# Five Strassen groups behind the keys and nine filler chunks in a written-out second attention

## The reference

```python
h = rms_norm(x, norm1_g)
q, k, v, bg, cg, xc = split(h @ w_in)            # 6 x 1024 columns
y_attn = chunked_relpos_attention(q, k, v, ...)  # 16 heads of 64, chunks of 64,
                                                 # each sees itself and 8 earlier ones
y_conv = bg * (conv_b + causal width-3 conv of cg * xc)
gates  = sigmoid(h @ w_gate + b_gate)            # 2 x 1024 columns
x = x + (g_attn * (y_attn @ w_attn_proj) + g_conv * (y_conv @ w_conv_proj)) @ w_out
```

## Time and profile before

| | before |
|---|---|
| runs | 2168.96, 2170.98, 2181.47 us, median 2170.98 |
| the profiled execution | 2173.93 us, span 2172.1 us |
| PE busy | 2145.6 us, 99% |
| DVE, ACT, POOL busy | 1472.0, 949.6, 998.3 us |
| instructions | 29103 |

### The profile page before, as it was taken

One profiled execution on the slowest core, in us unless ns is written; L12 is line 12 of the kernel. 1 busy time (PEld: TensorE's weight loads), 2 busy tenths in 40 slices (PEclk: granted clock), 3 DMA queues, 4 the chain that ended last, 5 costly groups with the idle time before them and its releaser, 6 DMA issues.

```text
span 2172.1 us, 29103 instructions
## 1 busy us (share of the span) xinstructions
PE 2145.6 (99%) x10450; PEld 1788.2 (82%) x10450; DVE 1472.0 (68%) x2585; ACT 949.6 (44%) x1696; POOL 998.3 (46%) x701
## 2 busy tenths in 40 slices
PE   8999999999998999999999999999999999999999
PEld 8888888888887888888888888788878887888887
DVE  7776775265874666666666658543776777898886
ACT  5555425343342555555555531212555454433332
POOL 3232465454644131322223147457466565556564
PEclk9999999999999999999999999999999999999999
DMA  7320124332226332323333256315143545826433
GB/s 231 105 76 21 45 91 152 126 117 97 87 88 176 89 108 69 112 72 104 88 93 88 69 195 241 107 49 194 49 154 140 171 146 185 319 93 228 150 122 115
DMA packets 198606, 269.34 MB, mean 124 GB/s; under 512 B 58136, under 2 KB 116280, under 8 KB 198368
## 3 DMA queue, kind: packets, MB, share of 16 engines
q1 hardware_dynamic: 124880, 201.38, 27.5%
q10 hardware_dynamic: 73616, 66.49, 10.0%
HBM read 191.23 MB, written 85.00 MB: 127 GB/s over the span
## 4 chain that ended last, share of the span: by engine, by line
PE 76%; DVE 9%; ACT 5%; DMA 4%; issue 4%; POOL 1%; ACTq 1%; DVEq 0%; SPq 0%; POOLq 0%
PE ps L204 64%; PE ps L2379 3%; DMA w_raw<-in_w_up_dram 2%; PE ps L2354 2%; PE ps L2366 2%; DVE res L3476 1%; DVE mlp_acc L3476 1%; PE ps L776 1%; DMA u_parts<-res 1%; PE ps L751 1%; PE ps L762 1%; DVE k_lo L2599 1%; ACT w_hi L3323 1%; DVE a_lo L446 1%; DVE mlp_acc L3464 1%
## 5 line engine op out<-in xcount | busy, mean ns | idle before, releaser
L204 PE MATMUL ps<-a_hi,w_hi 128*128 128x512 f32 x1376 | 536.9, 407 | 7.4 <-DVE res L2149 5.1
L159 POOL TENSOR_TENSOR w_hi<-w_raw,zero 128x512 fp32r<-128x512 f32 x172 | 203.5, 1214 | 735.6 <-PE ps L204 604.9
L204 PE MATMUL ps<-a_hi,w_lo 128*128 128x512 f32 x1376 | 516.6, 392 | 0.0
L204 PE MATMUL ps<-a_lo,w_hi 128*128 128x512 f32 x1376 | 514.0, 390 | 0.0
L204 PE MATMUL ps<-w_hi,a_hi 128*128 128x512 f32 (+1 forms) x960 | 368.5, 384 | 4.1 <-POOL w_lo L672 2.2
L204 PE MATMUL ps<-w_hi,a_lo 128*128 128x512 f32 (+1 forms) x960 | 367.1, 382 | 0.0
L204 PE MATMUL ps<-w_lo,a_hi 128*128 128x512 f32 (+1 forms) x960 | 366.8, 382 | 0.0
L204 PEld LDWEIGHTS ps<-a_hi,w_lo 128*128 128x128 f32 x1376 | 258.4, 188 | 57.7
L204 PEld LDWEIGHTS ps<-a_hi,w_hi 128*128 128x128 f32 x1376 | 258.8, 188 | 50.8 <-POOL w_lo L1923 5.5
L204 PEld LDWEIGHTS ps<-a_lo,w_hi 128*128 128x128 f32 x1376 | 259.8, 189 | 40.8
L164 POOL TENSOR_TENSOR w_lo<-w_raw,w_hi 128x512 fp32r<-128x512 f32 x172 | 243.4, 1446 | 3.4
(11 more groups left out here) (307 smaller groups left out, 3929.9 us busy)
## 6 DMA issues: line engine op xcount, KB each, us to landing
mlp_part<-u_parts SPq DMA_DIRECT2D x26, 1024.0 KB, 7.9
w_raw<-in_w_in_dram SPq DMA_DIRECT2D x24, 1024.0 KB, 5.3
feat_fm<-stage ACTq DMA_DIRECT2D x68, 256.0 KB, 2.1
u_parts<-mlp_acc SPq DMA_DIRECT2D x28, 512.0 KB, 2.8
u_parts<-res SPq DMA_DIRECT2D x28, 512.0 KB, 2.8
conv_in<-feat_fm ACTq DMA_DIRECT2D x24, 512.0 KB, 5.5
res<-in_x_dram SPq DMA_DIRECT2D x16, 512.0 KB, 6.4
w_raw<-in_w_out_dram SPq DMA_DIRECT2D x8, 1024.0 KB, 5.1
```

The costliest lines, as they stand in the source:

```text
L159: hi = nc.gpsimd.tensor_tensor(w_hi[slot][:, k:k + 2, :], w_raw[:, k:k + 2, :], zero[:, 0:1].unsqueeze(2).to_broadcast([P, 2, CW]), ALU.add)
L204: last = nc.tensor.matmul(out_of(o), lhs, rhs(o), start=first and n == 0, stop=final and n == 2)
```

## The change

`BCX_GROUPS` goes from 1 to 5, so that 2560 of the 3072 columns of bg, cg, xc are made by Strassen groups behind the keys, in `phase_qkv`, and two chunks of them are left. The attention gets a parameter `fill_chunks`, here 9: the two chunks and the first seven gate chunks. Behind the first chunk, its 32 products are spread evenly over all 130 steps, at 260 filler parts (`filled_to`). All eight pairs are written out instead of looped. On ACT the order in a step becomes: rounding of the turned row (`high`), exponential, store and copy of filler products (`STORE_AT`, `OUT_AT`), then as before. The merge stage begins with the same gate chunk.

```diff
-        BCX_GROUPS = 1
+        BCX_GROUPS = 5
+        FILL_CHUNKS = 9
         W_BCX2 = seg(io["w_in_2"], 0, 3072 + 512 * BCX_GROUPS, 12 - 2 * BCX_GROUPS)
...
-            TAIL = 2 * (STEPS + 2)
-
-            def tail_step(x):
-                return next(n for n in range(STEPS + 2) if 8 * KB * (2 * n + 2) // TAIL >= KB * (x + 1))
+            FILLED = 4 * (fill_chunks - 1)
+            PARTS = 2 * (STEPS * pairs + 2)
+
+            def filled_to(part):
+                return FILLED * KB * part // PARTS
+
+            def last_step(x):
+                return next(n for n in range(PARTS // 2) if filled_to(2 * n + 2) >= KB * (x + 1))
+
+            OUT_AT = {0: -1, **{last_step(x) + 1: x for x in range(FILLED)}}
+            STORE_AT = {n + 1: x for n, x in OUT_AT.items()}
...
-                feed(block, w_start, 2 * pairs + 1, lambda j: (mm_h, j * 4 + 4))
+                feed(block, w_start, fill_chunks, lambda j: (mm_h, j * 4 + 4))
...
-                def pair_loop(eng, body):
-                    body(0, True, False)
-                    with eng.Fori(0, pairs - 2) as j:
-                        body(j + 1, False, False)
-                    body(pairs - 1, False, True)
+                def pair_loop(body):
+                    for i in range(pairs):
+                        body(i, i == 0, i == pairs - 1)
...
-                    def product_part(i, n, h, last):
-                        part = 2 * n + h
-                        ends = (8 * KB * part // TAIL, 8 * KB * (part + 1) // TAIL) if last else (2 * part, 2 * part + 2)
-                        for x in range(ends[0] // KB, (ends[1] - 1) // KB + 1):
-                            ks = range(max(ends[0] - x * KB, 0), min(ends[1] - x * KB, KB))
-                            product(i * 2 + (w_start + 1 + x // 4), x, ks, i * 8 + (EARLY + x))
+                    def product_part(i, n, h):
+                        part = 2 * (STEPS * i + n) + h
+                        begin, end = filled_to(part), filled_to(part + 1)
+                        for x in range(begin // KB, (end + KB - 1) // KB):
+                            ks = range(max(begin - x * KB, 0), min(end - x * KB, KB))
+                            product(w_start + 1 + x // 4, x, ks, EARLY + x)
...
+                            high()
                             if n + 1 < STEPS or not last:
                                 exps(i, n + 1)
-                            if last and n >= 2:
-                                for x in range(8):
-                                    if n == tail_step(x) + 2:
-                                        product_store(i, x)
-                                    if n == tail_step(x) + 1:
-                                        product_out(i, x)
-                            elif n % 2 == 0:
-                                product_out(i, n // 2 - 1)
-                            else:
-                                product_store(i, n // 2 - 1)
-                            high()
+                            step = STEPS * i + n
+                            if step in STORE_AT:
+                                product_store(STORE_AT[step])
+                            if step in OUT_AT:
+                                product_out(OUT_AT[step])
                             if n % 2 and not (first and n < 2):
...
-            feat_stored, banks_read = phase_attention(8, qkv2, 0, 1024, 2048, 4, ext2, (io["q_norm_g_2"], io["k_norm_g_2"]), W_BCX2, feat2[512 * BCX_GROUPS:, :],
+            feat_stored, banks_read = phase_attention(8, qkv2, 0, 1024, 2048, 4, ext2, (io["q_norm_g_2"], io["k_norm_g_2"]), W_BCX2, FILL_CHUNKS, feat2[512 * BCX_GROUPS:, :],
                             banks_read, ready_first, ready_rest)
-            opened, banks_read = phase_merge(W_GATE + 5 + 2 * BCX_GROUPS, feat_stored, banks_read)
+            opened, banks_read = phase_merge(W_BCX2 + FILL_CHUNKS, feat_stored, banks_read)
```

More of the change, by code:

```diff
@@ L2249, in phase_qkv, with phase_attention @@
                     [store_q[0, 1].at(32), store_q[1, 1].at(32), b_store[0].at(16 * NG), b_store[1].at(16 * NG)])
-        def phase_attention(pairs, src, q_col, k_col, v_col, back, ext, norm_gains, w_start, dst, banks_read, ready_first, ready_rest):
+        def phase_attention(pairs, src, q_col, k_col, v_col, back, ext, norm_gains, w_start, fill_chunks, dst, banks_read, ready_first, ready_rest):
             nslot = back + 2
@@ L2262, in phase_attention @@
             EARLY = 4
-            TAIL = 2 * (STEPS + 2)
-            def tail_step(x):
-                return next(n for n in range(STEPS + 2) if 8 * KB * (2 * n + 2) // TAIL >= KB * (x + 1))
+            FILLED = 4 * (fill_chunks - 1)
[6 more added lines that the diff above has]
+            STORE_AT = {n + 1: x for n, x in OUT_AT.items()}
+            assert len(OUT_AT) == FILLED + 1
             S_BANK, PT_BANK, O_BANK, G_BANK, T_BANK = 0, 2, 4, 5, 7
@@ L2401, in product @@
                                 pe.wait_ge(split_done, chunk + 1)
-                            if isinstance(out_index, int) and out_index < 2:
+                            if out_index < 2:
                                 pe.wait_ge(*banks_read[out_index])
@@ L2432, in body @@
                         for n in range(STEPS + 2 if last else STEPS):
-                            product_part(i, n, 0, last)
+                            product_part(i, n, 0)
                             if first and n == 0:
@@ L2439, in body @@
                                 turn(i, n - 1)
-                            product_part(i, n, 1, last)
+                            product_part(i, n, 1)
                             if n + 2 < STEPS or not last:
@@ L2446, in body @@
                                 round_(i * 2 + (n // 8 + 1), n % 8 // 4)
-                    pair_loop(pe, body)
+                    pair_loop(body)
                 @block.scalar
@@ L2475, in v_high, with product_out, product_store @@
                         nc.scalar.activation(v_st[:, slot, :, 0:HD], v_raw[:, :, :], ACT.Copy).then_inc(hi_v, 1)
-                    def product_out(i, x):
-                        act.wait_ge(mm_h, i * 8 + (EARLY + x + 1))
-                        act.wait_ge(st_h[x % 2], (i * 4 + (EARLY + x) // 2 + 1) * 16)
+                    def product_out(x):
+                        act.wait_ge(mm_h, EARLY + x + 1)
+                        act.wait_ge(st_h[x % 2], ((EARLY + x) // 2 + 1) * 16)
                         nc.scalar.activation(stage[:, x % 2, :], ps[:, G_BANK + x % 2, :], ACT.Copy).then_inc(ev_h, 1)
[L2484 to L2488, removed]
+                    def product_store(x):
+                        act.wait_ge(ev_h, EARLY + x + 1)
+                        row = (EARLY + x) // 2 * P
+                        act.dma_start(dst[row:row + P, (x % 2) * 512:(x % 2 + 1) * 512], stage[:, x % 2, :]).then_inc(st_h[x % 2], 16)
                     for ready in ready_first:
@@ L2498, in _ @@
                     for r in range(2):
-                        product_out(0, r - EARLY)
-                        product_store(0, r - EARLY)
+                        product_out(r - EARLY)
+                        product_store(r - EARLY)
                         if r == 0:
@@ L2504, in _ @@
                     nc.scalar.activation(st[:, 3, 3:4], zero[:, 0:1], ACT.Exp)
-                    product_out(0, 2 - EARLY)
-                    product_store(0, 2 - EARLY)
+                    product_out(2 - EARLY)
+                    product_store(2 - EARLY)
                     act.wait_ge(lo_r, 3)
@@ L2569, in body @@
                                     load_head(i * 2 + (hh + 2))
[L2570 to L2575, removed]
+                    pair_loop(body)
+                    for x in range(FILLED):
+                        if last_step(x) + 1 >= PARTS // 2:
+                            product_out(x)
+                        if last_step(x) + 2 >= PARTS // 2:
+                            product_store(x)
                 @block.vector
@@ L2674, in body @@
                             link.close(PER)
-                    pair_loop(dve, body)
-            products = 8 * pairs + EARLY
-            return ([(st_h[s], 16 * (4 * pairs + EARLY // 2 + 1)) for s in range(2)],
+                    pair_loop(body)
+            products = FILLED + EARLY
+            return ([(st_h[s], 16 * (products // 2 + 1)) for s in range(2)],
                     [[(o_done, 8 * pairs + 1), (ev_h, products - 1)], [(ev_h, products), (lo_r, 4 * pairs + 1)],
```

## The result

The changed kernel took 2261.53 us (median of 4 runs, 2257.28 to 2263.73), the kernel before 2171.31 (4 runs). The ratio is 1.040, with a 95% interval of 1.037 to 1.044: 90 us slower, where 70 had been forecast.

The account below looks back on a forecast made before the run. TensorE, busy 99%, was taken as the bound, its filler covering a path through ACT and DVE. 153.2 - 6.5 - 76.3 = +70.4 us gave 2241 us against the median 2170.98, range 2188 to 2272.

Parts of the forecast that it names:

- R3: Rival, chance 0.16: waits in the attention pull TensorE's clock down, up to 25 us on top, 2266 us.
- Part 1: Four more Strassen groups behind the keys: +153.2 us, less 6.5 for the vanished stall.
- Part 2: Eight fewer filler chunks in the second attention: a head falls from 34.96 to 30.4 us, -76.3 us in all.
- (a): Row 2's turn to row 6's scores: path through ACT and DVE 6.4 us, PE work 3.4, wait 3.0 a head.
- (b): Row 4's turn to the next head's row 0 scores: path 4.8 us, PE work 3.7, wait 1.0.
- (c): PE waits 0.9 us for row 5's low half, behind ACT's rounding of the next head and of row 5.
- (d): Rows 6 and 7: waits for rounding and low half, and next-head loads on ACT's queue, together 1.4 us.
- (e): ACT's rounding of the next head stands ahead of row 2's rounding and delays it, 0.3 us taken.
- the stage: The second attention, forecast to save 76.3 us: 63.7 in 14 heads and 12.6 in the last pair.
- the last pair: The last two heads of the second attention: 71.9 us before, 59.3 forecast, saving 12.6.
- R1: Rival, chance 0.12: the chain is elastic, PE stays the bound, head 23.7 us, total 2138 us.
- R2: Rival, chance 0.12: only today's chain (a) shows, early rounding repays the rest; head 25.8 us, total 2173 us.

Follow-up runs that it names:

- e6: The changed kernel with two groups, 15 chunks and the split of e4: 2149.95 us, ratio 0.9899 to the kernel before.
- e2: The changed kernel with one group and 17 filler chunks as before, in the new code and order: 2173.70 us, ratio 1.0007 to the kernel before.
- e10: The changed kernel with one group, 17 chunks and the split of e4: 2157.65 us, ratio 0.9936 to the kernel before.
- e4: The changed kernel with DVE's lump (low halves of the next head's queries and keys) split, second half turned and rounded a step later: 2200.98 us.
- e1: The changed kernel with ACT's exponential of the next row ahead of the rounding again: 2275.17 us, ratio 1.0473 to the kernel before.
- e8: The changed kernel with row 5's row maximum taken on DVE before the next head's low halves, not after: 2248.12 us, ratio 1.0346 to the kernel before.
- e9: The changed kernel with two groups and 15 chunks, the next head's low halves unsplit: 2178.39 us, ratio 1.003 to the kernel before.
- e5: The changed kernel with three groups, 13 chunks and the split of e4: 2164.16 us, ratio 0.9962 to the kernel before.

## Why the prediction was right, and where not

The direction and its cause were right: the moved filler had been cover, and PE now waits where the walk said. The time lies in the range, but 20 us above the number, and 4 us above the band of 2205 to 2258 that the forecast itself had; it is nearer to R3's 2266.

Part 1: four groups less the stall were to cost 146.7 us, the first scores came 149.7 us later. In the changed kernel no wait of PE is listed from 640 us to the first scores but 0.5 us; the 5.06 us idle of the earlier trace rows is gone, as it is in e6, and it is still there in e2.

Part 2, path by path: (a) 6.4 forecast, 6.16 found, and 5.57 us of it are ACT's and DVE's. (a) and (b) together, 4.0 us a head, make 60 in 15 heads; the scores are listed with 57.7, and by the distances between starts they were 68 us late. (c), (d) and (e), 2.6 us a head, make 39; values, turns and rounds are listed with some 22 us, and by the distances they were 38 us late, 11 of which they had been before. So (a) and (b) were a little low, (c) to (e) too high, and the sum close: 99 forecast, 95 more than before found.

PE's own work was sized right: I took 0.23 us off for each filler matmul removed and got 23.7 us a head; at e10's pace the changed kernel has 369 us in 16 heads, 23.1 each. Taking the listed waits off misleads here. It leaves 545.3 us in e10 and 404.4 in e4, 0.184 for each of 768 matmuls removed, as if these gave back less than their pace. But filler matmuls start 0.23 us apart in e4 as in e10, and what grew is unlisted delay: from the last filler matmul to the scores it is 0.23 us in e10 and 0.40 in e4 (medians, idle time taken off).

The 20 us missing: the stage saved 57.3 instead of 76.3. Of these 19 us, 13 lie in the second to fourteenth head, which took 31.4 on average instead of 30.4; the four at full clock took 29.5 to 30.4, so it is the heads with falls that are longer. Another 3 lie in the first head, which I had priced like the others, though it took 31.1 before and 29.5 after, and 2.5 in the last pair (61.8 instead of 59.3). R3, which I had as a rival at 0.16 with up to 25 us, came true: its price, 16 to 25 us, is nearly the whole miss. **The forecast and R3 were not exclusive**, and the sum should have had a term for the clock, which it put at nothing. That the time is in the range all the same is due to its upper end, which had a loss of clock in it; the number had none. On the Trainium skill's rule ("TensorE: Matmul & The Clock Gate", section "HAM oscillation — how this bites in real kernels"), that waits between bursts make the clock fall in each round of a loop: the trace agrees in kind, but early on it was every other head, not each.

The ordering of ACT was read with the wrong sign. On path (a) it costs an exponential, as forecast, and e1 shows that the other paths gain more. I had priced only the path on which it hurts.

R1 (elastic, 2138) and R2 (2173) are refuted by the waits and the time. That the move of the filler and not the code was the cause is shown by e2; that the order on ACT and DVE decides how much the missing cover costs, by e1, e4 and e8. How much of e4's 60 us is the lump on DVE alone, and how much the second half's later turn and rounding, stays open; so do what sets off a fall of the clock, why the late heads have more of them, and whether another placing of the lump would carry three groups.

## What to carry to other kernels

Filler that keeps TensorE busy is also the cover of a path through other engines. Before taking it away, time that path from one PE instruction to the next that depends on it and compare it with the PE work in between; where the two are equal today, each matmul removed there comes back as a wait. Then look for a lump on the path that can be put in pieces elsewhere: here that was worth 60 us at five groups with no work removed. It also turned the move of the first group from a loss of 5 us (e2 to e9) into a gain of 8 (e10 to e6); of the 22 us that e6 gains on the kernel before, the split with one group (e10) gives the other 14. A list of waits is a lower bound: compare the starts of successive matmuls with their pace in a kernel that does not wait. An instruction moved for one path's sake must be priced on every path that it lies on.

## What was not expected of the hardware

PE at half clock: idle 2.77 us was followed by 3.2 us at 0.50, idle 2.55 us in the next head was not. But in e8 the clock fell 14 times with no wait over 1.5 us, and in e5 not once with one of 2.8 us. Plain matmuls of 512 columns start 0.23 us apart and are given 0.39 us each, so that the lists show 37 us of waiting in e4 where the starts show 70 us of delay.
